# Recurrence of the gated linear attention on one core: k with q and the product with v at full array width, and twenty unused products of x ahead of the scan

## What is computed

```python
def gla_chunk(S, q, k, v, loga):
    L = q.shape[1]
    b = jnp.cumsum(loga, axis=1)
    causal = jnp.tril(jnp.ones((L, L), dtype=bool))[None, :, :, None, None]
    decay = jnp.exp(jnp.where(causal, b[:, :, None] - b[:, None, :], NEG_INF))
    att = jnp.einsum('bthd,bshd,btshd->bhts', q, k, decay)
    o = jnp.einsum('bhts,bshv->bthv', att, v) + jnp.einsum('bthd,bhdv->bthv', q * jnp.exp(b), S)
    b_last = b[:, -1]
    S_new = S * jnp.exp(b_last)[..., None] + jnp.einsum('bshd,bshv->bhdv', k * jnp.exp(b_last[:, None] - b), v)
    return S_new, o
```

## Time and profile before

| | |
|---|---|
| median of 3 runs | 3795.69 us (3794.48 to 3796.97) |
| the profiled execution: time | 3794.63 us |
| the profiled execution: span | 3792.7 us |
| TensorE busy, whole span | 3515.1 us (93%) |
| VectorE, ScalarE, GpSimd busy | 1554.9, 1131.8, 584.8 us |
| mean granted clock | 0.948 |

### The profile page before, as it was taken

How to read it: one execution, slowest core, us unless ns; L and a number is a source line. 1 busy time by engine, 2 the same in 40 slices (tenths; PEclk the granted TensorE clock), 3 DMA queues, 4 the chain that set the end, 5 groups by cost and what they waited for, 6 DMA issues and landing times. The chain is left out here.

```text
span 3792.7 us, 61595 instructions
## 1 busy us (share of the span) xinstructions
PE 3515.1 (93%) x26522; PEld 3294.5 (87%) x26522; DVE 1554.9 (41%) x2533; ACT 1131.8 (30%) x2104; POOL 584.8 (15%) x704
## 2 busy tenths in 40 slices
PE   8899798999999999998899884776999999999998
PEld 8898678989999999995698784664998999999997
DVE  6345444344332232335236667455344332232233
ACT  6223234223221121225434521444323321121123
POOL 1000101001110110121211357320200210010012
PEclk9999858999999999998899997997999999999999
DMA  7422302201111111115646575955200111111111
GB/s 229 99 63 61 101 8 54 78 23 40 45 45 50 45 45 45 47 38 152 223 141 215 197 189 130 220 131 116 95 29 22 46 45 45 45 50 45 45 41 67
DMA packets 457373, 323.16 MB, mean 85 GB/s; under 512 B 105118, under 2 KB 435198, under 8 KB 453854
## 3 DMA queue, kind: packets, MB, share of 16 engines
q1 hardware_dynamic: 402858, 280.72, 25.8%
q10 hardware_dynamic: 43876, 18.99, 2.0%
q0 software_dynamic: 10368, 19.51, 1.6%
HBM read 232.29 MB, written 86.96 MB: 84 GB/s over the span
## 5 line engine op out<-in xcount | busy, mean ns | idle before, releaser
L83 PE MATMUL ps<-am_y,am_wh 128*128 128x352 f32 x4896 | 1178.0, 322 | 0.0
L83 PE MATMUL ps<-am_h,am_wh 128*128 128x352 f32 x3648 | 880.3, 324 | 1.1 <-DVE am_h L1395 1.1
L83 PEld LDWEIGHTS ps<-am_y,am_wh 128*128 128x128 f32 x4896 | 853.5, 188 | 1.3
L83 PE MATMUL ps<-am_y,am_wl 128*128 128x352 f32 x2448 | 789.7, 323 | 0.0
L83 PEld LDWEIGHTS ps<-am_h,am_wh 128*128 128x128 f32 x3648 | 633.0, 188 | 4.2 <-DVE am_h L1395 1.4
L83 PE MATMUL ps<-am_h,am_wl 128*128 128x352 f32 x1824 | 585.4, 321 | 0.0
L83 PEld LDWEIGHTS ps<-am_y,am_wl 128*128 128x128 f32 x2448 | 459.8, 188 | 0.0
L83 PEld LDWEIGHTS ps<-am_h,am_wl 128*128 128x128 f32 x1824 | 342.6, 188 | 0.0
L1482 POOL TENSOR_TENSOR am_silu<-am_silu,rs 128x352 f32<-128x352 f32 x132 | 126.5, 960 | 1234.3 <-ACT am_silu L1339 1234.3
L83 PE MATMUL ps<-rw_parts,rw_wh 128*128 128x352 f32 (+1 forms) x1152 | 289.1, 333 | 24.0 <-PEq L2510 13.1
L1071 DVE TENSOR_TENSOR x<-ps,x 128x352 f32<-128x352 f32 x240 | 125.8, 524 | 450.7 <-PE ps L83 441.7
(11 more groups left out here) (323 smaller groups left out, 4669.7 us busy)
## 6 DMA issues: line engine op xcount, KB each, us to landing
am_w<-in_ffn_w SPq DMA_DIRECT2D x120, 512.0 KB, 3.8
rw_ra_d<-tb_rk SPq DMA_DIRECT2D x8, 1056.0 KB, 8.0
rw_kbt_d<-tb_gk SPq DMA_DIRECT2D x8, 1056.0 KB, 3.9
rw_gg_d<-tb_gk SPq DMA_DIRECT2D x8, 1056.0 KB, 6.1
fr_w<-in_xa_wk SPq DMA_DIRECT2D x8, 1024.0 KB, 5.4
fr_w<-in_xa_wv SPq DMA_DIRECT2D x8, 1024.0 KB, 5.5
am_w<-in_xa_wq SPq DMA_DIRECT2D x16, 512.0 KB, 3.9
am_w<-in_xa_wo SPq DMA_DIRECT2D x16, 512.0 KB, 3.9
```

What stands on the lines that cost most here:

```text
L83: mm = nc.tensor.matmul(out, l, part, start=start and n == 0, stop=stop and n == 2)
```

## The change

k with q becomes one product for both pairs of heads, 128 columns to 128 partitions. The parts in which the pairs cross are not zero there, so the mask tile becomes 128 x 128, cleared by GpSimd, with the causal mask loaded in its two diagonal squares, and VectorE masks 128 columns. The product of v with the masked tile becomes one of all 128 rows. It starts the accumulation now, and the two products of the state follow it, all in one bank, each state product in its 64 columns; the waits for the masked tile and for ScalarE's copy of the last result stand ahead of it. The state products still wait for the state. Ahead of all this, TensorE has twenty products of 512 columns of `x` with the identity, to the bank of the totals; nothing reads them.

```diff
--- before.py
+++ after.py
@@ -90,7 +90,8 @@
     return lambda u, dst: [(dst, wk[:, :, ds(u * P + first, P)])]
 
 
-def gla(nc, ps, a, o, ab, gate, y, ones, ident):
+def gla(nc, ps, a, o, ab, gate, y, x, ones, ident):
+
 
 
 
@@ -102,8 +103,8 @@
         zz, q, k, t, l, c_ = (sb(s, 2, 2, BLK) for s in ("z", "q", "k", "t", "l", "c"))
         v, sg, vr = sb("v", 2, GLA_HEADS, BLK), sb("g", 2, GLA_HEADS, BLK), sb("vr", NCH, GLA_HEADS, C)
         qp, kp, dec = sb("qp", NCH, 2, 2, C), sb("kp", NCH, 2, 2, C), sb("dec", 2, NCH)
-        state, kv, g = sb("state", 4, 2, GLA_DV), sb("kv", 2, 2, P), sb("gm", 2, HD)
-        mask, keep, gain, eps, one = sb("mask", HD), sb("keep", BLK), sb("gain", 1), sb("eps", 1), sb("one", 1)
+        state, kv, g = sb("state", 4, 2, GLA_DV), sb("kv", 2, 2, P), sb("gm", 2, P)
+        mask, keep, gain, eps, one = sb("mask", P), sb("keep", BLK), sb("gain", 1), sb("eps", 1), sb("one", 1)
         sq, rsg = sb("sq", GLA_HEADS, BLK), sb("rs", GLA_HEADS, BLK)
         z_in, qk_in, v_in, g_in = ([sem(f"{s}_in{i}") for i in range(2)] for s in ("z", "qk", "v", "g"))
         mask_in, keep_in, gain_in, init_in, set_, cleared = (
@@ -152,7 +153,9 @@
                     sp.dma_start(dst[h], state[r, src]).then_inc(stored, 16)
 
             load(0)
-            sp.dma_start(mask[:], a["c_mask_gla"][:, 0:HD]).then_inc(mask_in, 16)
+            sp.wait_ge(set_, 3)
+            for r in halves:
+                sp.dma_start(mask[r, r], a["c_mask_gla"][r, r]).then_inc(mask_in, 16)
             init = a["state_gla"][0, 0].rearrange("(p h) a b -> h a p b", h=2)
             for h, r in enumerate(halves):
                 sp.dma_start(state[r, 2], init[h]).then_inc(init_in, 16)
@@ -172,6 +175,7 @@
         def _(pool):
             nc.gpsimd.memset(one[:], 1.0).then_inc(set_, 1)
             nc.gpsimd.memset(eps[:], EPS).then_inc(set_, 1)
+            nc.gpsimd.memset(mask[:], 0.0).then_inc(set_, 1)
             for tile in (kp, qp):
                 nc.gpsimd.memset(tile[:], 0.0).then_inc(cleared, 1)
             for b in range(BLOCKS):
@@ -207,10 +211,8 @@
                     pe.wait_ge(qp_set, 2 * b + 2)
                 if c:
                     pe.wait_ge(g_out, c)
-                for p, r in enumerate(halves):
-                    mm = nc.tensor.matmul(ps[r, G, 0:HD], kp[:, c, p].rearrange("r h t -> r (h t)"),
-                                          qp[:, c, p].rearrange("r h t -> r (h t)"), start=True, stop=True)
-                mm.then_inc(made, 1)
+                nc.tensor.matmul(ps[:, G, 0:P], kp[:, c].rearrange("r p h t -> r (p h t)"),
+                                 qp[:, c].rearrange("r p h t -> r (p h t)"), start=True, stop=True).then_inc(made, 1)
 
             def scan(c):
                 s = c % 2
@@ -220,18 +222,17 @@
                 for p, r in enumerate(halves):
                     mm = nc.tensor.matmul(ps[:, S + p, 0:GLA_DV], kv[r, s, 0, :], kv[r, s, 1, :], start=True, stop=True)
                 mm.then_inc(s_done, 1)
+                if c:
+                    pe.wait_ge(y_out, c)
+                pe.wait_ge(g_out, c + 1)
+                nc.tensor.matmul(ps[:, Y, 0:P], kv[:, s, 1, :], g[:, s, :], start=True, stop=False)
                 if c == NPC:
                     pe.wait_ge(init_in, 32)
                 else:
                     pe.wait_ge(state_ready, c + 1)
-                if c:
-                    pe.wait_ge(y_out, c)
                 for p in range(2):
-                    nc.tensor.matmul(ps[:, Y + p, 0:HD], state[:, old(c), p, :], qp[:, c, p].rearrange("r h t -> r (h t)"),
-                                     start=True, stop=False)
-                pe.wait_ge(g_out, c + 1)
-                for p, r in enumerate(halves):
-                    mm = nc.tensor.matmul(ps[:, Y + p, 0:HD], kv[r, s, 1, :], g[r, s, :], start=False, stop=True)
+                    mm = nc.tensor.matmul(ps[:, Y, p * HD:(p + 1) * HD], state[:, old(c), p, :],
+                                          qp[:, c, p].rearrange("r h t -> r (h t)"), start=False, stop=p == 1)
                 mm.then_inc(y_done, 1)
 
             def total(b, h, bank):
@@ -241,6 +242,8 @@
                     pe.wait_ge(logs, GLA_HEADS * b + h)
                 nc.tensor.matmul(ps[:, bank, 0:BLK], ones[:], sq[:, h], start=True, stop=True).then_inc(sums, 1)
 
+            for _ in range(20):
+                nc.tensor.matmul(ps[:, TOTAL, :], ident[:], x[:, 0, 0:512], start=True, stop=True)
             make(0)
             for c in range(NCH):
                 if c + 1 < NCH:
@@ -280,7 +283,7 @@
 
             def masked(c):
                 dve.wait_ge(made, c + 1)
-                nc.vector.tensor_tensor(g[:, c % 2], ps[:, G, 0:HD], mask[:], ALU.mult).then_inc(g_out, 1)
+                nc.vector.tensor_tensor(g[:, c % 2], ps[:, G, 0:P], mask[:], ALU.mult).then_inc(g_out, 1)
 
             def add(c):
                 dve.wait_ge(s_done, c + 1)
@@ -306,7 +309,7 @@
             nc.vector.memset(state[:, 0], 0.0).then_inc(state_ready, 1)
             cumulate(0)
             queries(0)
-            dve.wait_ge(mask_in, 16)
+            dve.wait_ge(mask_in, 32)
             masked(0)
             for c in range(NCH):
                 if c + 1 < NCH:
@@ -368,7 +371,7 @@
             def leave(c):
                 act.wait_ge(y_done, c + 1)
                 nc.scalar.activation(y[:, :, c * C:(c + 1) * C].rearrange("r (p h) t -> r p h t", h=2),
-                                     ps[:, Y:Y + 2, 0:HD].rearrange("r p (h t) -> r p h t", h=2), ACT.Copy,
+                                     ps[:, Y, 0:P].rearrange("r (p h t) -> r p h t", p=2, h=2), ACT.Copy,
                                      scale=GLA_DK ** -0.5).then_inc(y_out, 1)
 
             def square(b, h0, h1):
@@ -2966,7 +2969,7 @@
                 even_products(nc, ps, a, o, h, rs, ab, gate, yb, ident)
         ya = mix.enter_context(nc.sbuf_tensor("o_a", [P, 4, TOK], F32))
         with nc.cleanup_on_exit():
-            gla(nc, ps, a, o, ab, gate, ya, ones, ident)
+            gla(nc, ps, a, o, ab, gate, ya, x, ones, ident)
         wo = a["ab_w_out"][0]
 
         def load_out(u, dst):
```

## The result

The changed kernel took 3755.76 us (median of 4 runs, 3749.29 to 3760.83) against 3795.22 of the kernel before: a ratio of 0.9893, 95% interval 0.9881 to 0.9905. It is faster by 39.5 us; I had forecast 3784, and the low end of my range, 3757, lies 1.2 us above the median. The profiled execution took 3757.36 us, 37.3 less than the one of before, with a span of 3755.3.

The account below looks back on a forecast made before the run. TensorE at half clock was taken as the bound. Likeliest case: -5.6 to chunk 9 (start included), -0.7 before the fall, +3.2 for cold chunks, -8.8 after the clock's return, sum -11.9, so 3784 us; range 3757 to 3802.

Parts of the forecast that it names:

- Start: Before the scan: the twenty products delay the first transpose to 457.3, costing +3.7 us (+2.0 to +5.4).
- (a): Chunk 1 of blocks 0 and 1: TensorE waits 0.6 us for ScalarE's three activations and two copies.
- (b): Chunk 3: TensorE waits about 0.7 us for VectorE's accumulate and the work after it.
- rival 2: Whole scan: the clock holds to the end, the queries' wait being shorter; -36.5 us, 3759; chance 0.15.
- 2.55 us of full array: Beside totals: full-array work from a total to the end of k with q, against 1.9 before, returns the clock.
- (c): Chunk 6: queries take 3.6 us, TensorE waits 1.3 at k with q, then 0.5; the clock should fall.
- the likeliest case: Scan: clock falls at chunk 8 or 9, returns with block 2's totals; sum -11.9 us, 3784.
- 1.00 through the queries: Sign that the prediction is wrong: the clock stands at 1.00 through the queries, where 0.50 from about 480 was expected.
- A chunk at full clock: Each warm chunk of the scan takes 2.15 us (2.0 to 2.9), a gain of 1.27.
- +0.2 us a chunk: k with q at full width costs 0.2 us more per chunk at half clock (bounds 0 and +0.42).
- the state products after it are the same instructions: State products behind the value product: same instructions, the wait for ScalarE's copy only moves ahead; no difference.
- The slower side: Clock falls as soon as the scan begins or before chunk 3: 3806, or 3801 at chunk 2 or 3; chance 0.15.

Follow-up runs that it names:

- e4: Changed kernel, with VectorE's queries in block 0 made to wait for GpSimd's two k products: 3764.35 us, ratio 0.9923.
- e9: Changed kernel with sixteen products of x instead of twenty and k with q in two narrow products from chunk 1 on: 3766.12 us, ratio 0.993.
- e2: Changed kernel without the twenty products of x: 3765.56 us, ratio 0.9926.
- e10: Kernel before with the two narrow value products moved ahead of the state products, nothing else: 3772.01 us in one run.
- e5: Kernel before with k with q at full width and the mask's edits, no products of x: 3790.25 us, ratio 0.9994.
- e1: Kernel before with the twenty products of x added and nothing else: 3797.26 us, ratio 1.0007.
- e11: Changed kernel without products of x, k with q narrow from chunk 1 on, wide value product behind the state products: 3773.39 us in one run.
- e6: Changed kernel without products of x, k with q narrow from chunk 1 on, value product wide and ahead of the state: 3773.26 us, ratio 0.9954.
- e7: Changed kernel with sixteen products of x and the late normalization work cut into finer pieces: 3756.92 us, ratio 0.9914.
- e8: The changed kernel run again as it is: 3754.79 us, ratio 0.99.

## Why the prediction missed

**Right.** Start: +3.7, first transpose at 457.3; it came at 457.28 against 453.66. The products took 19.10 us, the clock was back at 441.9 where I had 442. The clock comes back beside totals: e4, e9, e2 and the changed kernel itself at 513.6. The waits (a) and (b), forecast as 0.6 and 0.7, were 0.93 and 0.96 (464.80 and 468.96), and the clock held over both. The mask's clear was 0.21 and cost nothing. Late pieces of ScalarE end the warm stretch in block 2. Waits within the scan: rival 2 had "some 8", and 7.4 were measured.

**Right, but not for the reason given.** The return was to come from "2.55 us of full array", a total with the transposes and the full k with q behind it. e9 has no full k with q there and e10 no widened product at all, and both came back; e5, with the full k with q alone, did so too, but only at 514.1 and for 10 us. Either edit is enough.

**Wrong, and it decides: the step "(c) Chunk 6: queries", "with 3.6 for them, 1.3 us of wait at k with q, and then 0.5".** The queries took 1.80 and the waits were 0.31 and 0.17. I had scaled from the cold trace, where the queries and GpSimd's k products take turns, and I took for granted that both would be released close together. They were, and the two engines began within 0.01 us (472.41 and 472.42), but VectorE was the first, so that GpSimd's copy of the decay took 0.94, not 0.22, and its k products began only at 473.51. By that the clock didn't fall at chunk 8 or 9, and the likeliest case with its sum of -11.9 was gone; the sign that I had named for being wrong, 1.00 through the queries, came. The size of the step was not bad for the other outcome: where GpSimd was first, queries took 3.2 and the waits were 1.01 and 0.64 (e1) or 1.68 (e9), against 1.3 and 0.5, and the clock fell. The rows of before that I read could not tell which of the two would come.

**Wrong in size: "A chunk at full clock", 2.15 us.** It was 1.68. I scaled update and state products by the transposes' 0.37/0.61, to 1.06; they took 0.81. The 0.37 was itself too long a price, since the second of its two transposes is on half of the columns: transposes, k with q and value product took 0.23, 0.31 and 0.33. In e1, whose chunk has the parts of before, it was 2.01 (459.88 to 461.89), close to my lower bound; the other 0.33 came with the new order and width.

**Wrong in sign: "+0.2 us a chunk" for k with q at half clock, and "the state products after it are the same instructions", at no difference.** It was -0.38. The 0.61 of the transposes that I took as the price of a full product held the change to narrow products behind them, 0.14, and part of that from the value product ahead. The wide k with q itself is even, e5 against before: it costs 0.14 and gives as much back at the transposes. The order, which I had costed at nothing because it only moved a wait, gives the gain: e10 alone saves 0.49 a chunk. The value product's width, costed at nothing too, saves 0.28 without the order (e11) and costs 0.10 with it (e6 against e10).

**The chance of rival 2, 0.15,** rested on (c) and on the thin mix of work. Its figure, 3759, lies 3 us from what came, by luck and by other terms: I had 33 x 1.27 and no cold chunks; a warm chunk gave 1.75, with some four chunks cold. From its first start to its last end the scan gained 48.0 us, 453.66 to 578.22 before and 457.28 to 533.83 after; what was given back behind it brought the two sums together. Whether an earlier warm scan has a part in those 7 us stays open: each kernel with products gained 4 to 10 us less in the median than by the start behind; of those without, e6 (26.5 against 20.1) and e11 did too, and e2, e5 and e10 did not.

**Slips that changed nothing.** 512 columns come to 0.42 us by rows 8, not 0.43; without a rise of the clock the first transpose would have come at 473, not 470; 3801 and 2 us make 3803, not 3802.

The slower side, a fall before chunk 3 after the products, came in no run, not even with narrow products.

## What to carry over

In a stage bound by small products, count the changes between full products and those on half the rows or columns before counting columns: grouping like with like took 0.5 of 3.4 us a chunk with no other edit. Warm-up products pay only if what follows holds the clock; tried alone they looked worthless, and with the other edits they added some 10 us. When a wait is priced from a trace where instructions of VectorE and GpSimd lengthen each other, check which of them will start first in the new order: here 0.01 us ahead or 0.03 behind was the difference between 1.80 and 3.22 us.

## What the runs showed of the hardware

- A change between full and half-array products costs 0.14 us at 1.2 GHz, and 0.05 to 0.17 more in the first products behind (e10, e11, e5 and the changed kernel against before).
- The same 2 x 704 columns took VectorE 1.80 us begun 0.01 us ahead of GpSimd's copy, 3.22 begun 0.03 behind it (e9), and 4.32 begun within the k products. GpSimd's copy took 0.94 in the first case and 0.22 in the second. A multiply of 0.58 took 2.00 (e7).
- The clock held over waits of 0.93, 0.96, 0.31 and 0.17 us in the changed kernel. It was lost behind 1.01 and 0.64 in e1, 1.12 and 0.58 in e5, 1.68 in e9 and 1.73 in e10. With the same waits to 0.01 us, the changed kernel fell in block 1 in one profile (503.3) and not in another (e8).
- The clock came back from 0.50 beside totals when k with q alone was full (e5) and when the order alone was changed (e10), and did not in the kernel before and in e1.
- A stretch of 1140 us that the change doesn't touch took 6 us more for the same work in another execution, with the mean clock 0.91, not 0.92.
